# Gate and up products of a SwiGLU block with the high and low part of x in one 512-column matmul

## The reference, cut to what matters

```
def swiglu(x, w_gate, w_up, w_down):
    return (jax.nn.silu(x @ w_gate) * (x @ w_up)) @ w_down

for l in range(DEPTH):                       # DEPTH = 2
    h = h + 0.5 * swiglu(rms_norm(h, ffn1_norm[l]), ffn1_gate[l], ffn1_up[l], ffn1_down[l])
    h = h + token_mixing(rms_norm(h, mix_norm[l]), w_in[l], ...)
    h = h + 0.5 * swiglu(rms_norm(h, ffn2_norm[l]), ffn2_gate[l], ffn2_up[l], ffn2_down[l])
return rms_norm(h, final_norm)
```

## Time and profile before

| what | value |
|---|---|
| median of 3 runs | 1044.88 us (1044.26 to 1046.57) |
| the profiled execution | 1045.52 us, span 1043.7 us |
| TensorE (PE) busy | 1016.2 us, 97% of the span, 7096 matmuls |
| weight loads (PEld) busy | 926.3 us, 89% |
| VectorE (DVE) busy | 709.4 us, 68% |
| ScalarE (ACT) busy | 495.9 us, 48% |
| chain that ended last | 91% TensorE, 3% issue, 3% VectorE |

### The profile page before, as it was taken

How to read it: one execution, slowest core, us unless ns; L and a number is a source line. 1 busy time by engine, 2 the same in 40 slices (tenths; PEclk the granted TensorE clock), 3 DMA queues, 4 the chain that set the end, 5 groups by cost and what they waited for, 6 DMA issues and landing times.

```text
span 1043.7 us, 19491 instructions
## 1 busy us (share of the span) xinstructions
PE 1016.2 (97%) x7096; PEld 926.3 (89%) x7096; DVE 709.4 (68%) x1405; ACT 495.9 (48%) x804; POOL 85.5 (8%) x120
## 2 busy tenths in 40 slices
PE   7999999999989999999989999999999999999996
PEld 7999999989867999999989999999897689999996
DVE  5766666679676766666577666666896767666665
ACT  6544444564545444444355444445745454444442
POOL 1000000010551000000010000000015500000000
PEclk9999999999999999999999999999999999999999
DMA  8855555544533555555446555554453446555541
GB/s 318 304 183 189 187 185 182 176 161 138 188 108 136 191 192 188 189 186 181 143 134 211 183 183 185 187 187 142 143 202 122 133 151 221 188 192 183 181 141 41
DMA packets 35873, 183.46 MB, mean 176 GB/s; under 512 B 3952, under 2 KB 6000, under 8 KB 21360
## 3 DMA queue, kind: packets, MB, share of 16 engines
q1 hardware_dynamic: 35824, 182.83, 52.3%
HBM read 180.19 MB, written 2.62 MB: 175 GB/s over the span
## 4 chain that ended last, share of the span: by engine, by line
PE 91%; issue 3%; DVE 3%; ACT 1%; POOL 1%; DVEq 0%; POOLq 0%; ACTq 0%
PE ps L516 28%; PE ps L518 27%; PE ps L517 27%; DVE wlo L916 1%; PE ps L527 1%; PE ps L528 1%; PE ps L531 1%; PE ps L694 1%; PE ps L706 1%; PE ps L555 1%; PE ps L685 1%; PE ps L681 1%; DVE wlo L922 0%; DVE X L964 0%; PE ps L563 0%
## 5 line engine op out<-in xcount | busy, mean ns | idle before, releaser
L516 PE MATMUL ps<-xhi,whi 128*128 128x256 f32 x1600 | 454.0, 284 | 0.0
L518 PE MATMUL ps<-xhi,wlo 128*128 128x256 f32 x1600 | 452.2, 283 | 0.0
L517 PE MATMUL ps<-xlo,whi 128*128 128x256 f32 x1600 | 451.8, 282 | 0.0
L516 PEld LDWEIGHTS ps<-xhi,whi 128*128 128x128 f32 x1600 | 306.0, 191 | 5.7 <-issue 2.0
L517 PEld LDWEIGHTS ps<-xlo,whi 128*128 128x128 f32 x1600 | 306.0, 191 | 3.8
L518 PEld LDWEIGHTS ps<-xhi,wlo 128*128 128x128 f32 x1600 | 306.1, 191 | 0.0
L916 DVE TENSOR_TENSOR wlo<-raw,whi 128x1024 fp32r<-128x1024 f32 (+2 forms) x224 | 261.1, 1203 | 9.2 <-ACT whi L313 7.2
L313 ACT CAST whi<-raw 128x1024 fp32r<-128x1024 f32 (+2 forms) x224 | 219.3, 1028 | 29.4 <-PE ps L518 27.2
L922 DVE TENSOR_TENSOR wlo<-raw,whi 128x1024 fp32r<-128x1024 f32 (+1 forms) x112 | 131.5, 1174 | 97.7 <-ACT whi L317 97.7
L346 ACT ACTIVATE sig<-hg 128x256 f32<-128x256 f32 x88 | 36.9, 419 | 273.0 <-DVE hg L981 273.0
L516 PE MATMUL ps<-whi,hhi 128*128 128x512 f32 x352 | 139.8, 397 | 0.4 <-DVE hlo L993 0.4
(11 more groups left out here) (146 smaller groups left out, 907.1 us busy)
## 6 DMA issues: line engine op xcount, KB each, us to landing
raw<-stream SPq DMA_DIRECT2D x112, 1024.0 KB, 5.2
raw<-stream SPq DMA_DIRECT2D x112, 512.0 KB, 3.6
table<-feat SPq DMA_DIRECT2D x1, 1536.0 KB, 12.7
cst<-consts SPq DMA_DIRECT2D x1, 1088.0 KB, 12.9
X<-x SPq DMA_DIRECT2D x2, 512.0 KB, 5.6
bias<-table SPq DMA_DIRECT2D x1, 1024.0 KB, 6.2
out<-feat SPq DMA_DIRECT2D x4, 256.0 KB, 2.1
fgain<-final_gain SPq DMA_DIRECT2D x1, 512.0 KB, 8.0
```

What stands on the lines that cost most here:

```text
L516: nc.tensor.matmul(out_, a[0], b[0], start=start, stop=False)
L517: nc.tensor.matmul(out_, a[0], b[1], start=False, stop=False)
L518: return nc.tensor.matmul(out_, a[1], b[0], start=False, stop=stop)
```

## The change

`xhi` and `xlo` become the two halves of one tile `xboth`, 512 columns for each k. For the steps f = 1 to 21 `three` is replaced by `wide`: one matmul of 512 columns with the high weights stationary and both halves of x moving, and one of 256 columns with the low weights and the high half. The high·low product therefore comes to lie in the right half of a PSUM bank and must be added to the left half afterwards. Gate and up have a bank each (4 + 2s and 5 + 2s). ScalarE copies the right half to SBUF (`glo`, `ulo`) and VectorE adds the left half (`gsum`, `usum`), before `rows` is multiplied in. The four lie in the tile `val`, which a SwiGLU block doesn't use, so rows of the order call them all `val`. `gate_mm` now counts in all steps. The broadcast of the norm's factors goes to bank 2 in the SwiGLU blocks (`ROWS_FFN`), and stays in bank 7 in the mixing block. Step 0 of each phase, `down`, and the mixing block's products keep their form.

```diff
-        xhi = sb("xhi", [P, KT, S], F32R)
-        xlo = sb("xlo", [P, KT, S], F32R)
+        xboth = sb("xboth", [P, KT, 2 * S], F32R)
+        xhi, xlo = xboth[:, :, 0:S], xboth[:, :, S:2 * S]
...
@@ ScalarE, step f
+                    bank = GU + 2 * s
+                    if f > 0:
+                        act.wait_ge(gate_mm, n + 1)
+                        nc.scalar.copy(glo[:, s, :], ps[:, bank, S:2 * S]).then_inc(glo_out, 1)
                     act.wait_ge(hg_out, n + 1)
                     nc.scalar.activation(sig[:, s, :], hg[:, s, :], ACT.Sigmoid).then_inc(sig_out, 1)
+                    if f > 0:
+                        act.wait_ge(front_done, n + 1)
+                        nc.scalar.copy(ulo[:, s, :], ps[:, bank + 1, S:2 * S]).then_inc(ulo_out, 1)
...
@@ TensorE
+            def wide(bank, a, k):
+                nc.tensor.matmul(ps[:, bank, :], a[0], xboth[:, k, :], start=k == 0, stop=False)
+                return nc.tensor.matmul(ps[:, bank, 0:S], a[1], xhi[:, k, :], start=False, stop=k == KT - 1)
...
-                    if f >= 3:
-                        pe.wait_ge(ur_out, n - 1)
                     for g in range(2):
+                        if f >= 3:
+                            pe.wait_ge((gsum_out, usum_out)[g], l * (2 * NF - 2) + i * 2 + (phase * (NF - 1) + f - 2))
                         front_here(l, k0 + f, i, g)
-                        to = ps[:, GU + s, g * S:(g + 1) * S]
...
-                            t = three(to, w(s, g * UNIT + k * P, P), xt(k), k == 0, k == KT - 1)
...
+                            t = wide(GU + 2 * s + g, w(s, g * UNIT + k * P, P), k)
+                        t.then_inc((gate_mm, front_done)[g], 1)
...
@@ VectorE, step f > 0
+                        dve.wait_ge(glo_out, m)
+                        nc.vector.tensor_tensor(gsum[:, s, :], ps[:, bank, 0:S], glo[:, s, :], ALU.add).then_inc(gsum_out, 1)
+                        dve.wait_ge(gsum_out, m)
+                        nc.vector.tensor_tensor(hg[:, s, :], gsum[:, s, :], rows[:, :], ALU.mult).then_inc(hg_out, 1)
                         dve.wait_ge(front_done, n + 1)
+                        dve.wait_ge(ulo_out, m)
+                        nc.vector.tensor_tensor(usum[:, s, :], ps[:, bank + 1, 0:S], ulo[:, s, :], ALU.add
+                                                ).then_inc(usum_out, 1)
+                        dve.wait_ge(sig_out, n + 1)
+                        nc.vector.tensor_tensor(ht[:, s, :], hg[:, s, :], sig[:, s, :], ALU.mult).then_inc(ht_out, 1)
+                        dve.wait_ge(usum_out, m)
+                        nc.vector.tensor_tensor(ur[:, s, :], usum[:, s, :], rows[:, :], ALU.mult).then_inc(ur_out, 1)
                     dve.wait_ge(ht_out, n + 1)
                     dve.wait_ge(ur_out, n + 1)
                     nc.vector.tensor_tensor(hf[:, s, :], ht[:, s, :], ur[:, s, :], ALU.mult).then_inc(h_out, 1)
```

More of the change, by code:

```diff
@@ L120, in trunk @@
         val = sb("val", [P, NB, D])
+        gsum, usum, glo, ulo = (val[:, i // 2, i % 2 * 512:i % 2 * 512 + 512].rearrange("p (a t) -> p a t", a=2)
+                                for i in range(4))
         wft = sb("wft", [2 * NH, S])
@@ L169, in trunk @@
         GU = 4
-        LASTUP = 7
-        ROWS = 7
+        ROWS_FFN, ROWS_MIX = 2, 7
         CB = 2
@@ L564, in spread, with spread_rows @@
                 return t
-            def spread_rows(n):
+            def spread_rows(n, bank):
                 pe.wait_ge(diag_out, n + 1)
-                spread(ROWS).then_inc(rows_mm, 1)
+                spread(bank).then_inc(rows_mm, 1)
             def ffn(l, phase):
@@ L578, in up @@
                         front_here(l, k0)
-                        first([(ps[:, g, 0:S], lambda k, g=g: w(0, g * UNIT + k * P, P)) for g in range(2)],
-                              l * (3 * KT) + 2 * phase * KT)[1].then_inc(front_done, 1)
+                        gate, up = first([(ps[:, g, 0:S], lambda k, g=g: w(0, g * UNIT + k * P, P)) for g in range(2)],
+                                         l * (3 * KT) + 2 * phase * KT)
+                        gate.then_inc(gate_mm, 1)
+                        up.then_inc(front_done, 1)
                         return
-                    if f >= 3:
-                        pe.wait_ge(ur_out, n - 1)
                     for g in range(2):
+                        if f >= 3:
+                            pe.wait_ge((gsum_out, usum_out)[g], l * (2 * NF - 2) + i * 2 + (phase * (NF - 1) + f - 2))
                         front_here(l, k0 + f, i, g)
-                        to = ps[:, GU + s, g * S:(g + 1) * S]
-                        if f == NF - 1 and g == 1:
-                            to = ps[:, LASTUP, 0:S]
                         for k in range(KT):
                             if f == 1 and g == 0 and k == KT // 2:
-                                spread_rows(l * 3 + 2 * phase)
-                            t = three(to, w(s, g * UNIT + k * P, P), xt(k), k == 0, k == KT - 1)
-                        if f == NF - 1 and g == 0:
-                            t.then_inc(gate_mm, 1)
-                    t.then_inc(front_done, 1)
+                                spread_rows(l * 3 + 2 * phase, ROWS_FFN)
+                            t = wide(GU + 2 * s + g, w(s, g * UNIT + k * P, P), k)
+                        t.then_inc((gate_mm, front_done)[g], 1)
                 def down(f, i=0):
@@ L736, in mix @@
                 u.then_inc(feat_mm, 1)
-                tile(QI, front(1, 0), 0, lambda: spread_rows(l * 3 + 1))
+                tile(QI, front(1, 0), 0, lambda: spread_rows(l * 3 + 1, ROWS_MIX))
                 tile(QI + 1, front(1), UNIT, token_major)
@@ L934, in mean, with norm @@
                                         ).then_inc(ms_out, 1)
-            def norm(n, g, l, k, first=False):
+            def norm(n, g, l, k, bank, first=False):
                 for t in range(KT):
@@ L957, in norm @@
                 dve.wait_ge(rows_mm, n + 1)
-                nc.vector.tensor_copy(rows[:, :], ps[:, ROWS, 0:S]).then_inc(rows_out, 1)
+                nc.vector.tensor_copy(rows[:, :], ps[:, bank, 0:S]).then_inc(rows_out, 1)
                 dve.wait_ge(rows_out, n + 1)
@@ L973, in step @@
                     s, n = f % 2, l * (2 * NF) + i * 2 + (phase * NF + f)
[L974 to L978, removed]
-                    else:
-                        dve.wait_ge(front_done, n + 1)
-                    nc.vector.tensor_tensor(hg[:, s, :], gate, rows[:, :], ALU.mult).then_inc(hg_out, 1)
@@ L982, in step @@
[L982 to L988, removed]
+                    dve.wait_ge(gate_mm, n + 1)
@@ L1223, in _ @@
                 split_front(l, 0)
-                norm(l * 3, G_FFN1, l, 1, first=True)
+                norm(l * 3, G_FFN1, l, 1, ROWS_FFN, first=True)
                 ffn(l, 0)
-                norm(l * 3 + 1, G_MIX, l, NF + 1)
+                norm(l * 3 + 1, G_MIX, l, NF + 1, ROWS_MIX)
                 mix(l)
-                norm(l * 3 + 2, G_FFN2, l, NF + MIXC + 1)
+                norm(l * 3 + 2, G_FFN2, l, NF + MIXC + 1, ROWS_FFN)
                 ffn(l, 1)
```

9 lines of the change are left out of this document (8 added, 1 removed).

## The result

The changed kernel took 1031.92 us in the median (1030.32 to 1033.06, 4 runs) against 1045.1 us (1044.26 to 1046.57, 4 runs): a ratio of 0.9871, 95% interval [0.9854, 0.9889], 13.2 us less. Forecast were 1035.6 and 9.3 less. The profiled execution took 1033.06, 12.5 less than the profiled one of before.

A forecast was written before the change was run, and what follows sets the result against it. TensorE's matmul pace was taken to bound the SwiGLU phases: 10.6 us saved in steps minus 1.3 at phase ends gives 9.3 less, 1036.2 profiled or 1035.6 on the median's scale; range 1031 to 1043.

The forecast's parts named there:

- TensorE sets the pace: SwiGLU phases: a step costs the distances between TensorE's matmul starts, 8.55 us before and 8.42 us after.
- the gain is what a step saves: Steps 1 to 21 of four phases: 0.126 us saved in each of 84 steps, 10.6 us.
- The narrow matmul behind a wide one: In each `up`: 256 columns following 512 cost 0.1167 us, as right behind a `down`, not 0.1200.
- a feed of pairs: In an `up`: matmul and load pairs are fed every 0.120 us; a `down` gives reserve for about eight matmuls.
- The size of this term: Each `up` of steps 1 to 21: 5.61 us instead of 5.74, saving 10.6 us in all.
- The rule of a fixed 2.5 ns per matmul: Joined matmuls in each `up`: a pair gives back only 2.5 ns, 3.4 us over 84 steps.
- The round: VectorE and ScalarE's elementwise work per step: 6.62 us grows by 1.42 to 8.04, staying below TensorE's 8.42.
- the reserve: Between `hlo` and the `down` needing it: each step adds 0.38 us, where before it was about 1.93.
- the phase end: Last step of each phase: down(21) waits 0.33 us for `hlo`, 1.3 us over four phases.
- the round waits for `back_done`: Within a phase: 0.38 us a step builds the reserve until elementwise work waits for TensorE's product again.
- The slower rival: Every step from f = 1: elementwise work takes 8.67 us and becomes the bound, about 1056 us; chance 0.09.

The follow-up runs named there:

- wide_only: Changed kernel's wide matmuls with the elementwise step of the kernel before, without the added copies and additions; 1032.35 us, ratio 0.9873.
- cols128: Kernel before, with 128 instead of 256 moving columns in steps 1 to 21, half of gate and up not computed; 1011.38 us, one execution.
- load64: Kernel before, with weight blocks of 64 stationary columns in steps 1 to 21, upper 64 rows not computed; 1018.76 us, one execution.
- end_order: Changed kernel, but in each phase's last step VectorE multiplies `hg`, `sig` and `rows` while waiting for the up product; 1031.5 us.
- both_early: Changed kernel with both copies before the sigmoid and both additions before `hg` in steps 1 to 20, last step reordered too; 1034.37 us, ratio 0.9875.
- extra_op: Changed kernel with one more 256-column VectorE copy, which nobody waits for, in steps 1 to 20; 1049.95 us, ratio 1.0054.
- wide_128: Changed kernel with 128 instead of 256 columns in the narrow matmul, half of the low-high product not computed; 1032.96 us, one execution.
- after_again: Changed kernel run once more, unaltered, against the kernel before; 1031.44 us, ratio 0.9861.
- after_c: Changed kernel run again, unaltered, on a third chip, against the kernel before; 1032.75 us, ratio 0.9877.
- adds_only: Kernel before's three narrow matmuls, with the change's copies and additions, left half added to itself; 1048.52 us, ratio 1.0026.
- both_early_b: both_early a second time, beside the unaltered changed kernel on a third chip; 1029.56 us, ratio 0.9864.

## Why the prediction was right, point by point

- TensorE sets the pace and the gain is what a step saves, taken over all steps: right. The matmuls without the additions keep all of the gain (wide_only), the additions without the matmuls cost 2.7 us.
- The narrow matmul behind a wide one costs about 0.117 and not 0.120: right, 0.116. The reason given, a feed of pairs that a `down` fills up for a while, was wrong in form. The size of the load plays a part: 0.111 is the floor with a 128-column load (cols128), and with a 64-column load 256 columns take 0.1136 (load64). In a row of 256-column matmuls the two are nearly equal, and together they give 0.120. Why that is 0.006 above the larger of them isn't explained. Nor is it explained why the wide one takes 0.231, a little below the 0.2342 read from the earlier trace rows (0.2338 over the whole trace).
- The size of this term was too small. An `up` of 5.61 was forecast and 5.552 came, and before it took 5.735. The steps and up(1) together gave 16.5 us, where the prediction had 10.6.
- The rule of a fixed 2.5 ns per matmul, which the prediction drew from the Trainium skill (TensorE: Matmul & The Clock Gate, "Back-to-back issue gap") with 3.4 us of gain, is against the trace: a joined pair of narrow ones gave 0.240 - 0.231 = 9 ns.
- The round: 8.04 forecast, 8.15 measured; 3.78 from `gsum` to `hlo` instead of 3.68. Most of that is one hop: from `ur` to `hf` it is 0.53 (181.31 to 181.84 on VectorE), and 0.46 was taken. The round stays under TensorE's pace, as forecast. But TensorE's pace came out at 8.35, so the reserve grows by 0.2 a step and not by 0.38.
- The step that was off is the phase end, which cost twice the forecast, 2.6 us instead of 1.3. The excess has three parts. First, the piece behind the up product takes 0.11 more than forecast, and the `down` that hides it is 0.01 shorter, in all four phases. This shows bare in phases 2 and 4. Second, the first matmul after the wait takes 0.10 more, also in all four; the prediction had no such term. Third, in phases 1 and 3, where VectorE has the first chunk of the next block to split, the whole round is late. There down(21) waits for a full round: 7.75 (190.88 to 198.63) less the `down` of 2.79 less the reserve of 4.3 (down(20) at 195.65, `hlo`(20) ready at 191.36) is 0.7, as seen. This adds 0.22 and 0.17 to the 0.56. The prediction took for granted that the round waits for `back_done` long before the end; 20 steps at 0.2 don't bring the reserve there. end_order and both_early tell the piece and the round apart.
- The slower rival was placed in every step. extra_op and wide_128 show that it is first paid at the ends of phases, and there in part twice.
- What no step held: the low clock at the start of the profiled execution, 1.7 us on TensorE of which 0.9 was left at down(0), and the 0.4 us behind the last matmul.
- The number was helped by luck. The steps gave 5.9 us more than forecast, the ends, the start and the rest took 2.8 us more. The forecast of 9.3 is therefore off by 3.1 in the profiled execution, and not by 5.9.

## What to carry to other kernels

A matmul's weight load is hidden as long as the matmul before it streams long enough. In this kernel 256 columns just about hid a load of 128, at 4 ns a matmul, and 128 columns didn't. Joining two matmuls that share a stationary operand paid here because load and stream were nearly equally long. When an elementwise chain has a round near that of the matmuls, look at the last step of the loop: with no more matmuls to cover it, it pays for the reserve that was not built. wide_128 shows the price. Its steps saved 8.1 us more, and the ends cost 8.4 more.

## What the runs showed of the hardware that was not expected

The granted clock reads 1.00 in the changed kernel from 15 to 19 us while the distances are those of 1.2 GHz (0.213 for 256 columns). From 524 to 526 us, in the same execution, the same distances stand beside a granted clock of 0.56. At the first place the row can't be trusted, and the distance can. The start of one of the kernels without the change:

```profile
15.07 0.58 PE L527 MATMUL ps<-xhi,whi 128*128 128x256 f32 x1 [0.61 <-ACT xhi L332]
15.45 0.41 PE L528 MATMUL ps<-xhi,wlo 128*128 128x256 f32 x1
15.66 0.41 PE L527 MATMUL ps<-xhi,whi 128*128 128x256 f32 x1
```

This is load64, whose matmuls there are those of the kernel before. Of the thirteen profiles, such a start is in after, after_again, after_c, wide_only, both_early, cols128 and load64, and not in before, adds_only, end_order, both_early_b, extra_op and wide_128. That is five of nine with the change and two of four without it. So it isn't tied to the change. The idle time ahead of it doesn't decide it either: 0.61 us in before and 0.61 in load64. What does is open. With the stretch the first down(0) of the changed kernel and its variants starts at 28.7 to 29.3, without it at 28.0 to 28.4, which accounts for part of the spread of the times. The second place, at the start of the third phase, is in the kernel before too (530.2 to 533.4, after 3.08 us of idle; in the changed kernel after 2.71).

A 256-column copy from SBUF to SBUF on VectorE took 0.28 us and added 0.20 to the round, where an addition or product of two tiles took 0.42 and added 0.33.
